# Ten homes for the weights of the first expert, and loads of the last expert that wait for TensorE

## The reference

```python
def moe_swiglu(h, router, wg, wu, wd):
    ...
    logits = jnp.einsum('td,de->te', ht, router).astype(jnp.float32)
    top_vals, top_idx = lax.top_k(logits, TOP_K)
    gates = jax.nn.softmax(top_vals, axis=-1)
    ...
    for e in range(N_EXPERTS):
        out = out + dense_gate[:, e:e + 1] * swiglu(ht, wg[e], wu[e], wd[e])
```

## Time and profile before

| | |
|---|---|
| median of three runs | 1376.38 us (1376.19 to 1377.13) |
| the profiled execution, its own time | 1376.21 us |
| its span, first to last instruction | 1374.4 us |
| TensorE matmul busy | 1338.8 us, 97% |
| DMA, mean rate over the span | 296 GB/s |
| mean granted TensorE clock | 0.992 |

### The profile page before, as it was taken

How to read it: one execution, slowest core, us unless ns; L and a number is a source line. 1 busy time by engine, 2 the same in 40 slices (tenths; PEclk the granted TensorE clock), 3 DMA queues, 4 the chain that set the end, 5 groups by cost and what they waited for, 6 DMA issues and landing times.

```text
span 1374.4 us, 32413 instructions
## 1 busy us (share of the span) xinstructions
PE 1338.8 (97%) x14781; PEld 932.3 (68%) x14781; DVE 513.2 (37%) x838; ACT 380.1 (28%) x515; POOL 97.7 (7%) x154
## 2 busy tenths in 40 slices
PE   6999999999999999999999999999989899999998
PEld 6879999888764545545455454554636878798896
DVE  6976555459761102001020010100101365647755
ACT  5664434344621000000000000000000256645643
POOL 3400000025004000000000000000012110000000
PEclk9999999999999999999999999999989999999999
DMA  9568785347579999999999999999999944343251
GB/s 327 185 229 279 275 297 184 124 147 232 181 289 385 409 413 410 415 410 411 414 408 415 410 411 405 408 415 396 409 394 394 346 156 138 111 149 125 93 184 61
DMA packets 124902, 407.03 MB, mean 296 GB/s; under 512 B 7490, under 2 KB 38722, under 8 KB 124768
## 3 DMA queue, kind: packets, MB, share of 16 engines
q1 hardware_dynamic: 116112, 389.57, 74.0%
q0 software_dynamic: 5792, 12.52, 2.9%
q10 hardware_dynamic: 2864, 2.88, 0.6%
HBM read 396.71 MB, written 16.12 MB: 300 GB/s over the span
## 4 chain that ended last, share of the span: by engine, by line
PE 82%; DVE 8%; DMA 7%; issue 1%; ACT 1%; DVEq 0%; SPq 0%; ACTq 0%
PE ps L2656 44%; PE ps L501 7%; PE ps L503 7%; PE ps L502 7%; DVE yT L2002 3%; PE ps L1186 2%; DMA ering<-in_moe_wu 2%; PE ps L1188 2%; PE ps L1187 2%; DVE low L491 2%; DMA ering<-in_moe_wd 2%; DMA ering<-in_moe_wg 2%; DMA rawb<-in_w_in 1%; PE ps L1395 1%; PE ps L1393 1%
## 5 line engine op out<-in xcount | busy, mean ns | idle before, releaser
L2656 PE MATMUL ps<-ering,xe 128*32 128x384 f32 (+1 forms) x6144 | 460.9, 462 | 7.0 <-issue 6.5
L2656 PEld LDWEIGHTS ps<-ering,xe 128*32 128x32 f32 x6144 | 208.0, 110 | 257.1 <-issue 157.7
L2656 PE MATMUL ps<-ering,eT 128*32 128x256 f32 x4224 | 230.0, 379 | 0.6 <-DMA ering<-in_moe_wd 0.6
L2173 DVE TENSOR_TENSOR eh<-eh,ps 128x384 f32<-128x384 f32 (+1 forms) x48 | 22.1, 516 | 523.8 <-PE ps L2656 523.8
L2656 PEld LDWEIGHTS ps<-ering,eT 128*32 128x32 f32 x4224 | 152.5, 110 | 77.5 <-issue 1.4
L491 DVE TENSOR_TENSOR low<-raw,high 128x2048 fp32r<-128x2048 f32 (+3 forms) x48 | 128.8, 2684 | 64.1 <-ACT high L486 62.9
L486 ACT ACTIVATE high<-raw 128x2048 fp32r<-128x2048 f32 (+3 forms) x47 | 105.5, 2244 | 91.5 <-PE ps L503 76.1
L501 PE MATMUL ps<-high,xT_hi 128*128 128x352 f32 (+1 forms) x368 | 128.2, 348 | 1.2 <-DVE xT_lo L2084 1.2
L503 PE MATMUL ps<-high,xT_lo 128*128 128x352 f32 (+1 forms) x368 | 127.1, 345 | 0.0
L502 PE MATMUL ps<-low,xT_hi 128*128 128x352 f32 (+1 forms) x368 | 126.8, 345 | 0.0
L1865 ACT ACTIVATE eh<-ps 128x384 f32<-128x384 f32 (+1 forms) x48 | 18.8, 464 | 330.3 <-PE ps L2656 330.3
(11 more groups left out here) (427 smaller groups left out, 1661.1 us busy)
## 6 DMA issues: line engine op xcount, KB each, us to landing
ering<-in_moe_wd SPq DMA_DIRECT2D x48, 1536.0 KB, 18.4
ering<-in_moe_wg SPq DMA_DIRECT2D x32, 1536.0 KB, 18.4
ering<-in_moe_wu SPq DMA_DIRECT2D x32, 1536.0 KB, 20.6
ering<-in_moe_wg SPq DMA_DIRECT2D x32, 1280.0 KB, 18.2
ering<-in_moe_wu SPq DMA_DIRECT2D x32, 1280.0 KB, 16.5
rawb<-in_w_in SPq DMA_DIRECT2D x25, 1024.0 KB, 5.0
raw<-in_w_in SPq DMA_DIRECT2D x16, 1024.0 KB, 8.8
ering<-in_moe_wd SPq DMA_DIRECT2D x16, 1024.0 KB, 19.2
```

Source lines behind the costliest of these rows:

```text
L2656: mm = nc.tensor.matmul(out_of(rows), tokens, columns_of(s), start=begins, stop=ends, skip_group_check=True)
```

## The change

Item 0's chunks 8 and 9 get homes outside the ring: `aside_y`, behind the ring's eight slots, and `aside_x`, over the transposed activations, which are free once the router's logits are made. Chunk 10 then goes to slot 0, and so on. Chunks 10 to 17 of item 0 wait for the chunk ten before; chunks 18 to 23 for the one eight before, as they did. Item 1 starts at slot 0 again, whose last user is now chunk 18 of item 0; its chunks 0 to 5 wait for two chunks more than before (`after += 2`). From its chunk 6 on the waits are the old ones. Landings in the aside homes are counted on the semaphores of the first loads of x.

In the last item, SP waits before chunk 3 (HELD_FROM) until TensorE has done the first four matmuls of that item (`last_begun`). Item 1's loads are now written out and no longer part of the loop.

```diff
@@ -157,6 +157,8 @@
+    aside = [nc.alloc_sbuf_tensor_at("aside_y", [P, 1, SLOT], F32, offset=ring_at + ESLOTS * SLOT * 4),
+             nc.alloc_sbuf_tensor_at("aside_x", [P, 1, SLOT], F32, offset=at[0])]
@@ -354,6 +356,8 @@
+    last_begun = sem("last_begun")
+    aside_landed, ASIDE_BEFORE = x_landed, 16
@@ -443,24 +447,50 @@
     wd_v = a["moe_wd"].rearrange("l e f n -> (l e) f n")
     DOWN_TILES = ((0, 1, 2), (3, 4, 5), (6, 7, 8), (9, 10, 11), (12, 13, 14), (15, 16, 17), (18, 19), (20, 21))
 
+    LEAD, HELD_FROM = ESLOTS + 2, 3
+
+    def is_first(i):
+        return isinstance(i, int) and i == 0
+
+    def home(first, j):
+
+        if not first or j < ESLOTS:
+            return ering, j % ESLOTS
+        if j < LEAD:
+            return aside[j - ESLOTS], 0
+        return ering, (j - LEAD) % ESLOTS
+
+    def landing(first, j):
+        if first and ESLOTS <= j < LEAD:
+            return aside_landed[j - ESLOTS]
+        return e_landed[home(first, j)[1]]
+
     def landed(i, j):
 
-        before = 16 * MOE0 // RAWS if j % ESLOTS < RAWS else 0
+        first = is_first(i)
+        if first and ESLOTS <= j < LEAD:
+            return ASIDE_BEFORE + 16
+        s = home(first, j)[1]
+        before = 16 * MOE0 // RAWS if s < RAWS else 0
+        if first:
+            return before + 16 * (1 if j < ESLOTS else (j - LEAD) // ESLOTS + 2)
+        if s >= ESLOTS - 2:
+            before -= 16
         return before + 16 * (j // ESLOTS + 1) + i * (16 * (FFN_CHUNKS // ESLOTS))
 
-    def load_expert(sp, e, j):
-
-        s = j % ESLOTS
+    def load_expert(sp, first, e, j):
+
+        ring, s = home(first, j)
         if j < 16:
             piece, up, k = j // 8, j // 4 % 2, 2 * (j % 4)
             width = STRIPS * WIDE[piece]
-            target = slot_view(ering, s, 2, width)
+            target = slot_view(ring, s, 2, width)
             source = (wg_v, wu_v)[up][e, :, k:k + 2, piece * PIECE0:piece * PIECE0 + width]
         else:
             t = DOWN_TILES[j - 16]
-            target = slot_view(ering, s, len(t), D)
+            target = slot_view(ring, s, len(t), D)
             source = wd_v[e, t[0] * P:(t[-1] + 1) * P, :].rearrange("(t p) n -> p t n", p=P)
-        sp.dma_start(target, source).then_inc(e_landed[s], 16)
+        sp.dma_start(target, source).then_inc(landing(first, j), 16)
 
     def chunk(i, j):
 
@@ -1554,8 +1584,13 @@
                 for j in range(FFN_CHUNKS):
                     if j == 12 and not last:
                         load_tokens(i)
-                    sp.wait_ge(w_used, chunk(i, j - ESLOTS + 1))
-                    load_expert(sp, e, j)
+                    after = j - ESLOTS + 1
+                    if isinstance(i, int) and j < ESLOTS - 2:
+                        after += 2
+                    if last and j == HELD_FROM:
+                        sp.wait_ge(last_begun, 1)
+                    sp.wait_ge(w_used, chunk(i, after))
+                    load_expert(sp, False, e, j)
 
             for j in range(FFN_CHUNKS):
                 if j == 22:
@@ -1564,10 +1599,17 @@
                     sp.wait_ge(lo_made, MOE0 - RAWS + j + 1)
                 elif j < ESLOTS:
                     sp.wait_ge(w_used, MOE0 - SPLITS + (1, 2, 3, 1)[j - RAWS])
+                elif j == ESLOTS:
+                    sp.wait_ge(w_used, MOE0 - SPLITS + 2)
+                elif j < LEAD:
+                    sp.wait_ge(logits_ready, 1)
+                elif j < LEAD + ESLOTS:
+                    sp.wait_ge(w_used, chunk(0, j - LEAD + 1))
                 else:
                     sp.wait_ge(w_used, chunk(0, j - ESLOTS + 1))
-                load_expert(sp, 0, j)
-            with sp.Fori(1, NE - 1) as i:
+                load_expert(sp, True, 0, j)
+            load_item(1, 1)
+            with sp.Fori(2, NE - 1) as i:
                 load_item(i, i)
             sp.wait_ge(routed, 1)
             last = sp.value_load(plan[0:1, LAST_COL:LAST_COL + 1], min_val=NE - 1, max_val=ITEMS - 1)
...
+                        if last and j == 0 and k == 0 and t == 0:
+                            mm.then_inc(last_begun, 1)
                 return mm
...
-                    pe.wait_ge(e_landed[j % ESLOTS], landed(i, j))
-                    gate_or_up(j, first).then_inc(w_used, 1)
+                    pe.wait_ge(landing(first, j), landed(i, j))
+                    gate_or_up(j, first, last).then_inc(w_used, 1)
```

More of the change, by code:

```diff
@@ L2663, in out_of, with gate_or_up @@
                 return lambda rows: ps[rows, bank, 0:WIDE[piece]].rearrange("p (b q) -> p b q", q=STRIP)
-            def gate_or_up(j, first):
+            def gate_or_up(j, first, last):
                 piece, up = j // 8, j // 4 % 2
                 n = WIDE[piece]
-                w = slot_view(ering, j % ESLOTS, 2, STRIPS * n)
+                w = slot_view(*home(first, j), 2, STRIPS * n)
                 for k in range(2):
@@ L2675, in gate_or_up, with down @@
                                        kt == 0, kt == KT - 1)
-                return mm
-            def down(j, t, n, tile):
-                w = slot_view(ering, j % ESLOTS, len(DOWN_TILES[j - 16]), D)
-                first = t % 2 * DOWN_N
-                return by_strips(lambda rows: ps[rows, 6 + t // 2, first:first + DOWN_N], eT[:, tile, STRIP * t:STRIP * t + STRIP],
+                        if last and j == 0 and k == 0 and t == 0:
+                            mm.then_inc(last_begun, 1)
+                return mm
+            def down(j, first, t, n, tile):
+                w = slot_view(*home(first, j), len(DOWN_TILES[j - 16]), D)
+                at_col = t % 2 * DOWN_N
+                return by_strips(lambda rows: ps[rows, 6 + t // 2, at_col:at_col + DOWN_N], eT[:, tile, STRIP * t:STRIP * t + STRIP],
                                  lambda s: w[:, n, DOWN_N * s:DOWN_N * s + DOWN_N], tile == 0 and t != 1, tile == FT - 1)
             def item(i, last=False):
-                first = isinstance(i, int) and i == 0
+                first = is_first(i)
                 for j in range(16):
@@ L2710, in item @@
                             for n, tile in enumerate(DOWN_TILES[j - 16]):
-                                mm = down(j, t, n, tile)
+                                mm = down(j, first, t, n, tile)
                             if t:
```

## The result

The changed kernel takes 1382.18 us (median of 7 runs, 1380.01 to 1382.56) beside 1377.13 us of the kernel before in the same session (7 runs, 1376.19 to 1378.58): a ratio of 1.0039, 95% interval 1.003 to 1.0049. It is slower by about 5.4 us (4.1 to 6.7 by the interval), and the prediction (1376.6, in a range of 1373.2 to 1378.6) was wrong. The profiled execution took 1382.31 us with a span of 1380.5, 6.1 us more than before.

The account below looks back on a forecast made before the run. The DMA stream of loads was taken to end the expert stage, behind TensorE. Homes +0.2, hold 0 and fetch 0 on the profiled 1376.21 us gave 1376.4, or 1376.6 us on the median's basis; range 1373.2 to 1378.6.

Parts of the forecast that it names:

- What bounds the kernel: End of the expert stage: the DMA stream ends it, 3.4 us behind TensorE; eo waits behind the third rawb load.
- Two more homes: Item 0's start: two loads fill idle DMA from 398 to 404, leaving 6.4 us less to load for item 0.
- What item 1 gives back: Item 1's first six loads wait longer, DMA runs dry 466 to 470; head start worth 0 to -0.6 us, taken as -0.2.
- The hold: Item 7's start: chunk 3 issued near 1005.3 instead of 986.8; DMA idle for 0, at most 0.5 us.
- The fetch: Item 7's start: first code-fetch pause stays, second of 1.47 us may shrink by up to 0.8; nothing on the path.
- The sum: Whole kernel: homes +0.2, hold +0.0, fetch 0 on the path, giving 1376.6 us; no change given 0.74.
- hold starves DMA: Item 7's start: late first products leave the queue dry, delaying rawb; 1379.3 us, chance 0.10 together with disturbed routing.
- The lead survives: After item 1: DMA stays 6.4 us ahead, rawb lands earlier, seam 4.6 us sooner; 1371.8 us, chance 0.16, whole or good part.

Follow-up runs that it names:

- e2: Kernel before with only the wait ahead of item 7's chunk 3 added, eight homes: 1377.75 us, ratio 1.0008.
- r8: Kernel before, item 1's first load waiting two chunks more and its second one more, so three loads are issued together: 1378.63 us, ratio 1.0012.
- r7: The changed kernel itself measured once more, against the kernel before: 1382.94 us, ratio 1.004.
- r9: Ten homes, item 1 starting in slot 6 so every later load waits eight chunks, plus the hold, against the kernel before: 1376.45 us, ratio 0.9999.
- e4: Ten homes, no hold, item 1 starting in slot 6 so every later load waits eight chunks, against the kernel before: 1372.67 us, ratio 0.9973.
- r4: Ten homes with the turned ring, no hold, against the kernel before in a session at 1390: 1393.94 us, ratio 1.0029.

## Why the prediction was wrong

*What bounds the kernel.* Right, and the experiments lean on it. ScalarE's eo started 3.4 us behind the third rawb in every trace of a session at 1376 with the old order, and TensorE's 4 us at item 7 (e2) counted for nothing.

*Two more homes.* Right in kind: (0,8) was issued at 386.0 and (0,9) at 393.2, DMA was full from 397 to 402. The lead was smaller than I had it: (0,22) landed 4.1 us earlier, where I had 5.4 to 6.4. The queue ran empty ahead of (0,18), as I had allowed, but for more than the 1 us: the share is 0.49 from 440 to 444.

*What item 1 gives back.* **This step failed, in its last part.** The issue at 469.6 and the landing of (1,0) came as predicted, within 0.1 us. The error is the sentence "(1,1) to (1,5) follow at the pace of use": a transfer of 3.8 us every 3.9 us was taken to leave no gap. It gave the term 0 to 0.6 us; measured are 2.4 to 3.6 us at (1,6) without the hold, and a ratio of 1.0026 to 1.0028, 3.6 to 3.8 us. Of this the empty stretch accounts for the 0.3 to 0.9 us at (1,0) and for most of r8's 1.7 us; the rest, some 2 us, is the shallow queue. What happens in it, the packet records of the changed kernel suggest: from 470 to 472 the packets of 6144 bytes take 396 ns in the mean and up to 1049, against 238 in the same stretch of before, and from 475.2 to 476.1 only 7 or 8 packets are under way on the 16 engines. So the engines seem to end a load at different moments, and they begin the next one slowly. r8 has slow packets behind its gap too, but from 473 on it is back at 234 to 246 ns, where the changed kernel stays at 250 to 310 from 475 to 483. That r8 gets back about half of the loss in time, and two thirds of it at (1,6), by three issues in a row is shown; which of the two, slow packets or unequal ends, costs how much is not.

The Trainium skill, "DMA: Bandwidth & Descriptors", section "Anatomy of one DMA — SWDGE (gpsimd) path", gives a transfer that GpSimd issues a fixed cost of about 2 us beside its data. The trace has the same size for a load that SP issues: (1,0), alone, took 6.1 us for 3.8 us of data. The prediction had this cost, by its rows of 6.2 and 5.7 us, and it doesn't explain the loss: with 6.1 us each (1,1) would have landed at 479.6, and it landed at 482.3.

*The hold.* **This step failed too**, in its size: the term was 0, at most 0.5 us. The step went by the last bytes of (7,2), and took the held load to be issued before them. In the changed kernel it was issued at 1011.09 and not at 1005.3, for three reasons: the stream was 3.3 us late already; TensorE, which had lived on those landings, ended item 6 at 1004.44, 4.8 us later than before; and SP issued 1.6 us after TensorE's first product, where I had counted 0.7. A lone load needs 6.1 us, so (7,3) can have landed at 1017.2 at the earliest; without the hold it would have been near 1014.9 (before 1007.8 and a transfer of 3.8, with the 3.3 late). That makes at least 2.3 us of the 2.9 by which the lateness grows from (7,0) to the third rawb. The landing itself is known in r7, the same kernel: 7.4 us after the issue, with four more loads issued right behind it. By the same working it is 3.3 us late there, and the lateness from (7,0) to the third rawb grows by 2.7, so the held load accounts for all of it. The hold alone costs 1.7 us by the same two columns (e2), in r9 4.1; by the times it is 1.1 us (e2, not told from nothing) and 1.8 us (changed less e1).

*The fetch.* The first pause stayed at 4.9 to 5.2 us in every trace, whatever the queue held. The second, 1.2 to 2.0 us, vanished with the hold in every trace and stayed in every one without it. I had given the hold at most 0.8 us of it; the whole of it went, and part of the stretch at half clock behind it: (7,0) is used up 11.9 us after item 6's end, not 15.0. That it would be off the path was right. The prediction weighed the rule of the Trainium skill ("DMA: Bandwidth & Descriptors", section "Queues, rings and completion order") that an engine takes turns between its queues, packet by packet, and concluded that the hold would give nothing. The pause went, but the traces don't speak against the rule: it is about queues that have work, and here the queue of the weights was drained (a share of 0.11 from 1010 to 1012). The conclusion missed that. Whether the depth of a queue that still has work matters to a fetch no run here shows.

*The sum and the rivals.* Homes +3.3 and hold +2.9 us make the +6.2 at rawb, against +0.2 and 0. The rival "hold starves DMA" had the right sign and place for the smaller part of it, at a chance of 0.10, and named the spread of the engines as its cause; but it needed a branch of 9 us, and the branch stayed at 6.2. "The lead survives" was ruled out correctly for this change, and is what e4 gets.

## What to carry to other kernels

A stream that is as long as the compute beside it has to be judged by its queue depth, not by whether each load is issued before it is due: a gap, and then loads issued singly at the pace of use, cost 3.8 us where the same gap with three loads behind it cost 1.7. A buffer added at the front gives time only if every later load keeps its distance; turning the ring (e4) turned a loss of 3.6 us into a gain of 3.7 in the sessions at 1376. But who frees a slot later delays all who wait for it: there the next block's loads and conversions came later, which made the same kernel slower at 1390 (r4). A pause put down to "issue" can be a wait; r4's was found in the order of VectorE's program. And a faster engine ahead of a seam is worth nothing while a transfer ends last there: the hold's 4 us on TensorE cost 1 to 4 us on the queue.

## What was not expected of the hardware

- One and the same kernel, on one and the same chip, has a level of 1376.4 and one of 1390.0 us in different sessions, and runs stay within 0.3% of either. The difference is made between 420 and 441, where TensorE stands still in 8 to 15 pieces of 0.2 to 1.6 us put down to "issue" and its products are slow. A change can be worth 0.9973 at one level and 1.0029 at the other.
- When loads came one by one behind a gap, DMA was back at 400 GB/s only from 483 on, thirteen us behind the first issue; when three came together it was there at 475, under five us behind it.
- When the stream of loads was held, half of the 16 engines seem to have run out some nine us before the others, judged by the count of packets (seven to nine packets under way from 1000.5 to 1008.5 in the changed kernel, sixteen before).
- The branch over the optional items took TensorE's sequencer 6.0 to 6.3 us and its first pause was 4.9 to 5.2 us, with a full queue and with a drained one. "Runtime: NRT & Kernel Launch" in the Trainium skill, section "Instruction fetch mechanics", says that a taken branch outside the prefetched pages forces a fetch by DMA before execution goes on. The constant pause agrees. That the second pause, which went when the queue was drained, is the fetch of the next block is likely by this, but no run shows it.
